# Trunk step: dispatch without the shift, shift added after the row turn, scatters issued back to back, and another layout for the last combination

## The reference

```python
mp = modulation(c_ctx[None, :], ada_w[l], ada_b[l])
ms = modulation(c, ada_w[l], ada_b[l])
...
hp = modulate(rms_norm(xp, norm_ffn[l]), mp[3], mp[4])
hs = modulate(rms_norm(xs, norm_ffn[l]), ms[3], ms[4])
xp = xp + mp[5] * hier_moe(hp, *moe)
xs = xs + ms[5] * hier_moe(hs, *moe)
```

## Time and profile before

| what | value |
|---|---|
| median of three runs | 1394.41 us |
| time of the profiled execution | 1396.16 us |
| its span | 1394.3 us |
| PE busy | 1235.7 us, 89% |
| DVE, ACT, POOL busy | 549.2, 380.5, 414.4 us |
| mean granted TensorE clock | 0.942 |
| DMA | 324.77 MB, mean 233 GB/s |

### The profile page before, as it was taken

One profiled execution on the slowest core, in us unless ns is written; L12 is line 12 of the kernel. 1 busy time (PEld: TensorE's weight loads), 2 busy tenths in 40 slices (PEclk: granted clock), 3 DMA queues, 4 the chain that ended last, 5 costly groups with the idle time before them and its releaser, 6 DMA issues.

```text
span 1394.3 us, 21214 instructions
## 1 busy us (share of the span) xinstructions
PE 1235.7 (89%) x7039; PEld 797.8 (57%) x7040; DVE 549.2 (39%) x1254; ACT 380.5 (27%) x779; POOL 414.4 (30%) x741
## 2 busy tenths in 40 slices
PE   6999998989989579998784899999999399999877
PEld 5666777655567345554443766665676255555437
DVE  3121424676622732222111449998213622222214
ACT  2210036556511311111110345664313011111110
POOL 0300100300000334453333159986001324445420
PEclk9999999989999779999997899999799599999998
DMA  9775653010036569999984911113552689999965
GB/s 379 269 255 210 260 216 134 3 61 1 1 39 233 228 261 411 423 424 423 423 356 173 273 58 38 57 61 102 116 205 112 261 334 408 369 421 423 423 247 227
DMA packets 104678, 324.77 MB, mean 233 GB/s; under 512 B 20405, under 2 KB 54171, under 8 KB 82083
## 3 DMA queue, kind: packets, MB, share of 16 engines
q1 hardware_dynamic: 84016, 290.36, 53.9%
q0 software_dynamic: 12464, 21.91, 4.4%
q10 hardware_dynamic: 8131, 11.59, 2.3%
HBM read 314.52 MB, written 27.10 MB: 245 GB/s over the span
## 4 chain that ended last, share of the span: by engine, by line
PE 65%; SPq 9%; DMA 9%; DVE 7%; issue 5%; ACT 2%; POOL 2%; ACTq 0%; POOLq 0%; DVEq 0%
PE PS L687 10%; PE PS L1043 10%; PE PS L1170 10%; PE PS L733 8%; PE PS L1065 5%; SPq L548 4%; DMA arena<-in_moe_w_up 4%; SPq L551 3%; PE PS L1111 3%; PE PS L640 3%; DVE scratch L1645 3%; PE PS L919 3%; DMA ring<-in_ada_w 2%; PE PS L1028 2%; DMA ring<-in_moe_w_up 2%
## 5 line engine op out<-in xcount | busy, mean ns | idle before, releaser
L1645 DVE TENSOR_TENSOR arena<-arena,PS 128x128 f32<-128x128 f32 (+3 forms) x109 | 40.3, 386 | 299.7 <-ACT arena L1540 288.8
L1043 PE MATMUL PS<-ring,arena 128*64 128x256 f32 x1088 | 132.3, 395 | 15.1 <-DMA ring<-in_moe_w_up 13.3
L733 PE MATMUL PS<-ring,arena 128*128 128x256 f32 (+1 forms) x640 | 143.3, 378 | 1.7 <-ACT arena L1352 1.7
L1170 PE MATMUL PS<-arena,ring 128*128 128x320 f32 x512 | 141.7, 438 | 3.5 <-issue 2.2
L1043 PE MATMUL PS<-arena 128*64 128x256 f32 x1120 | 130.6, 383 | 15.3 <-DMA arena<-in_moe_w_up 14.2
L2424 POOL TENSOR_TENSOR arena<-arena 128x655 f32<-128x655 f32 x91 | 129.7, 1425 | 45.2 <-ACT arena L1611 32.1
L687 PE MATMUL PS<-arena,ring 128*128 128x320 f32 x512 | 138.3, 433 | 4.8 <-DVE arena L1933 3.7
L733 PEld LDWEIGHTS PS<-ring,arena 128*128 128x128 f32 x640 | 116.3, 193 | 30.1 <-issue 15.3
L1170 PEld LDWEIGHTS PS<-arena,ring 128*128 128x128 f32 x512 | 97.7, 192 | 47.3 <-issue 8.6
L687 PEld LDWEIGHTS PS<-arena,ring 128*128 128x128 f32 x512 | 97.1, 190 | 45.6 <-issue 5.4
L2185 DVE SCALAR_TENSOR_TENSOR PS<-arena,vecT,PS 128x655 f32<-128x655 f32 x124 | 112.1, 904 | 4.2
(11 more groups left out here) (342 smaller groups left out, 1633.9 us busy)
## 6 DMA issues: line engine op xcount, KB each, us to landing
ring<-in_moe_w_up SPq DMA_DIRECT2D x64, 1024.0 KB, 15.1
arena<-in_moe_w_up SPq DMA_DIRECT2D x64, 1024.0 KB, 18.3
ring<-in_ada_w SPq DMA_DIRECT2D x48, 1024.0 KB, 9.0
ring<-in_moe_w_down SPq DMA_DIRECT2D x32, 1024.0 KB, 16.2
arena<-in_moe_w_down SPq DMA_DIRECT2D x32, 1024.0 KB, 18.5
arena<-y_rows ACTq DMA_DIRECT2D x10, 1024.0 KB, 8.0
ring<-in_od_w_in SPq DMA_DIRECT2D x16, 512.0 KB, 6.3
ring<-in_ev_w_in SPq DMA_DIRECT2D x7, 1024.0 KB, 15.6
```

The costliest lines, as they stand in the source:

```text
L733: last = pe.matmul(z_bank(i)[:, 0:n], hT[:, k, t * P:t * P + P], w[:, k, 0:n], start=(k == 0), stop=(k == KD - 1))
L1043: last = pe.matmul(PS[i * BLK:(i + 1) * BLK, 0, 0:2 * P].rearrange("p (a n) -> p a n", a=2), xblk[:, k, :], w[:, k % 4, :, i * P:(i + 1) * P],
L1170: last = pe.matmul(PS[:, 2 * a + n, 0:SEG], w[:, k, a, :], hT[:, k, n * SEG:(n + 1) * SEG], start=(k == 0), stop=(k == KD - 1))
L1645: return dve.tensor_tensor(out, a, b, op)
```

## The change

- *Dispatch.* Rows are sent without the latent shift, straight from ACT's `htok`. The latent shift, loaded as 128x8 values (`shift_x`), is added where DVE takes the turned rows (`take_rows`; one tensor_tensor for the copy). Context rows need the difference of the two shifts: DVE computes it (`shift_delta`), it goes to all partitions as one row (`delta_row`), and PE adds it to the context tile as a fifth product of its two halves, with a diagonal `cdiag` that ACT makes from the root. For these halves the turns become float32 products. POOL's five additions are gone.
- *Logits.* `router_bias` is gone. The two shift vectors stand as two more columns of `xA` (ACT copies them), pass with the raw logits, and two more selecting products give the biases; DVE forms `lbias` in the routing chain.
- *Scatters.* In POOL's loop the column copies come first, the gather no longer waits for the result block, and fewer small operations stand before a scatter. Before the last four scatters one copy takes all four columns, and the waits between them are gone.
- *First combination.* ACT squares by halves of a tile; POOL adds the eight chunks in three steps for four of the five tiles (the last is still summed by PE); sums, diagonals and spreads come one tile later in the order.
- *Last combination.* Tokens stay on partitions. PE turns `xT` while the results are awaited, and DVE copies it to `xout`, now in `ring`. Gate rows come through DRAM (`gate_rows`: two stores by element, two loads to all partitions). Per tile PE combines the lower 512 columns (two products of 512), ACT and DVE the upper ones, and DVE multiplies by the gate and adds.

The diff, cut to its core:

```diff
-            sp.wait_ge(ev("mod_c"), MODC + 5)
...
-                    .then_inc(ev("shift_dma"), 16)
+            sp.wait_ge(ev("coef"), DELTA[l])
+            for c, src in enumerate((modT[:, l, 24:24 + KD, 0], delta[:, l, :])):
+                sp.dma_start(shift_rows[2 * l + c].rearrange("(k p) -> p k", p=P), src,
+                             allow_slow_non_contiguous=True).then_inc(ev("shift_dma"), 16)
         if e == 2:
             sp.wait_ge(ev("shift_dma"), 64 * l + 32)
-            for c in range(2):
-                sp.dma_start(shift[c], shift_rows[2 * l + c].partition_broadcast(P)).then_inc(ev("shift_dma"), 16)
+            sp.dma_start(shift_x[:, :].rearrange("p (h m) -> p h m", h=2),
+                         shift_rows[2 * l].rearrange("(h p m) -> p h m", h=2, m=4)).then_inc(ev("shift_dma"), 16)
+            sp.dma_start(delta_row, shift_rows[2 * l + 1].partition_broadcast(P)).then_inc(ev("shift_dma"), 16)
         if e == NPLACE - 2:
             for t in range(NT):
-                sp.wait_ge(ev("h_tok"), NT * l + t + 1)
+                sp.wait_ge(ev("htok_a"), 2 * NT * l + 2 * (t + 1))
...
+for c in range(2):
+    sp.dma_start(gate_rows[c].rearrange("(k p) -> p k", p=P), modT[:, 1, 40:40 + KD, c],
+                 allow_slow_non_contiguous=True).then_inc(ev("shift_dma"), 16)
+sp.wait_ge(ev("down_mm1"), expert_done(EXPERTS - NPLACE))
+sp.wait_ge(ev("shift_dma"), 2 * 64 + 32)
+for c in range(2):
+    sp.dma_start(gate_row[:, c, :], gate_rows[c].partition_broadcast(P)).then_inc(ev("shift_dma"), 16)
 for s, t in enumerate(TILES):
-    sp.wait_ge(ev("xt_v"), 2 * NT + s + 1)
-    sp.wait_ge(ev("xt_a"), s + 1)
+    sp.wait_ge(ev("comb"), 2 * NT + s + 1)
...
-def router_bias(l, b):
...
-    last.then_inc(ev("shift_mm"), 1)
...
+            last = pe.matmul(PS[i:i + c, 2 * n, 0:SEG + 2 * n], wr_flat[:, ROUTE * k:ROUTE * k + c],
+                             xA[:, k, n * SEG:SEG + n * (SEG + 2)], start=(m == 0), stop=(m == KD // 2 - 1))
...
+        for c in range(2):
+            last = pe.matmul(PS[:, 6, (NT + c) * ROUTE:(NT + c + 1) * ROUTE], bc(rs[0:PAIR, T + c:T + c + 1], [PAIR, P]),
+                             cst[0:PAIR, C_SEL:C_SEL + ROUTE], start=True, stop=True)
...
+            rows = xA[:, 4 * half + j, cols(t)]
+            if t < ST:
+                last = pe.transpose(quad(b)[:, j, :], rows, ident)
+            else:
+                pe.matmul(quad(b)[:, j, :], rows, ident, start=(j == 0), stop=False)
+        if t == ST:
+            pe.wait_ge(ev("shift_dma"), 64 * (l + 1))
+            pe.wait_ge(ev("cdiag"), l + 1)
+            last = pe.matmul(PS[:, b, :], cdiag, delta_row[:, 512 * half:512 * half + 512], start=False, stop=True)
...
+        parts = KD if s == NT - 1 else 1
+        if parts == 1:
+            pe.wait_ge(ev("h_c"), SETUP + s + 1)
+        else:
+            pe.wait_ge(ev("squared"), KD + s + 1)
         if s >= 2:
             pe.wait_ge(ev("root"), ROOT[2] + s - 1)
-        for k in range(KD):
+        for k in range(parts):
             last = pe.matmul(PS[:, s % 2, 0:1], hT[:, k, cols(TILES[s])], ones[:, 0:1],
-                             start=(k == 0), stop=(k == KD - 1))
+                             start=(k == 0), stop=(k == parts - 1))
...
+    def turn_x():
+        for i in range(2 * NT):
+            t, half = i // 2, i % 2
             if i >= 4:
-                pe.wait_ge(ev(("xt_v", "xt_a")[i % 2]), (2 * NT if i % 2 == 0 else 0) + (i - 4) // 2 + 1)
+                pe.wait_ge(ev("xt_v"), 2 * NT + i - 3)
             for j in range(4):
-                last = pe.transpose(quad(i % 4)[:, j, :], xT[:, 4 * half + j, cols(TILES[s])], ident)
+                last = pe.transpose(quad(4 + i % 4)[:, j, :], xT[:, 4 * half + j, cols(t)], ident)
             last.then_inc(ev("x_t"), 1)
 
-    for s in range(NT + 2):
+    def combine_rows(s):
+        t = TILES[s]
+        pe.wait_ge(ring_full[SLOTS + t], back_full[l, t])
+        if s == 0:
+            pe.wait_ge(ev("wdiag"), 2 * NT * (l + 1))
+            pe.wait_ge(ev("xt_v"), 4 * NT)
+        if s == 4:
+            pe.wait_ge(ev("comb"), 2 * NT + 1)
+        for a in range(2):
+            last = pe.matmul(PS[:, 4 + s % 4, :], wdiag[:, a, t, :], ygat[:, t, a, 0:512],
+                             start=(a == 0), stop=(a == 1))
+        last.then_inc(ev("comb_mm"), 1)
+    if l == 1:
+        turn_x()
+        for s in range(NT):
+            combine_rows(s)
+        return
+    for s in range(NT + 3):
         if s < NT:
             combine(s)
-        if l == 0:
...
-            turn_out(s - 1)
+        if 2 <= s <= NT + 1:
+            tile_sum(s - 2)
+        if s >= 3:
+            spread(s - 3)
...
+        if k == 0:
+            act.activation(xA[:, :, T:TW], modT[:, l, 24:24 + KD, :], ACT.Copy)
...
+    act.wait_ge(ev("root"), ROOT[q])
+    act.activation(cdiag, ident, ACT.Copy, scale=ss[:, 1, ST:ST + 1]).then_inc(ev("cdiag"), 1)
...
+    for s in range(NT + 2):
         if s < NT:
-            act.wait_ge(ev("comb"), 2 * s + 2)
...
-            act.activation(ss[:, 1, s - 1:s], PS[:, (s - 1) % 2, 0:1], ACT.Sqrt, bias=eps, scale=1.0 / D) \
+            for half in range(2):
+                ks = slice(4 * half, 4 * half + 4)
+                act.wait_ge(ev("comb"), 2 * s + half + 1)
+                ins = act.activation(hT[:, ks, cols(TILES[s])], xT[:, ks, cols(TILES[s])], ACT.Square)
+            ins.then_inc(ev("squared"), 1)
+        if s >= 2:
+            act.wait_ge(ev("sumsq"), s)
...
+    act.wait_ge(ring_full[SLOTS + t], back_full[1, t])
+    act.activation(ygat[:, t, 0, 512:D], ygat[:, t, 0, 512:D], ACT.Copy, scale=wtok[:, 0, t:t + 1]) \
+        .then_inc(ev("xt_a"), 1)
...
+def shift_delta(l):
+    tt(delta[:, l, :], modT[:, l, 24:24 + KD, 1], modT[:, l, 24:24 + KD, 0], ALU.subtract).then_inc(ev("coef"), 1)
...
+    tt(lbias, PS[:, 6, NT * ROUTE:(NT + 2) * ROUTE].rearrange("p (c n) -> p c n", c=2),
+       bc(rb[:, l, :].unsqueeze(1), [P, 2, ROUTE]), ALU.add)
...
-        dve.tensor_copy(xblk.rearrange("p (c m) n -> p m c n", c=2),
-                        quad(3).rearrange("p m (c n) -> p m c n", c=2)).then_inc(ev(f"xblk_c{l}"), 1)
+        tt(xblk.rearrange("p (c m) n -> p m c n", c=2), quad(3).rearrange("p m (c n) -> p m c n", c=2),
+           bc(shift_x[:, :].rearrange("p (c m) -> p m c", c=2).unsqueeze(3), [P, 4, 2, BLK]), ALU.add) \
+            .then_inc(ev(f"xblk_c{l}"), 1)
...
+    def take_x():
+        for i in range(2 * NT):
+            dve.wait_ge(ev("x_t"), TURNED + i + 1)
+            dve.tensor_copy(xout[:, i // 2, 512 * (i % 2):512 * (i % 2) + 512], PS[:, 4 + i % 4, :]) \
+                .then_inc(ev("xt_v"), 1)
+        dve.wait_ge(ev("xt_v"), 4 * NT)
+        dve.wait_ge(ev("shift_dma"), 2 * 64 + 64)
+    def rows_out(s):
+        t = TILES[s]
+        c = 0 if t < ST else 1
+        lower, upper = ygat[:, t, 0, 0:512], ygat[:, t, 1, 512:D]
+        dve.wait_ge(ev("xt_a"), s + 1)
+        dve.scalar_tensor_tensor(out=upper, in0=upper, scalar=wtok[:, 1, t:t + 1], in1=ygat[:, t, 0, 512:D],
+                                 op0=ALU.mult, op1=ALU.add)
+        dve.wait_ge(ev("comb_mm"), 2 * NT + s + 1)
+        link(tt(lower, PS[:, 4 + s % 4, :], gate_row[:, c, 0:512], ALU.mult))
+        tt(upper, upper, gate_row[:, c, 512:D], ALU.mult)
+        link(tt(xout[:, t, 0:512], xout[:, t, 0:512], lower, ALU.add))
+        tt(xout[:, t, 512:D], xout[:, t, 512:D], upper, ALU.add).then_inc(ev("comb"), 1)
+    if l == 1:
+        take_x()
+        for s in range(NT):
+            rows_out(s)
+        return
+    for s in range(NT + 4):
         if s < NT:
             residual(s)
-        if l == 0:
...
-            turned_out(s - 2)
+        if 4 <= s:
+            normed_tile(s - 4)
+        if 3 <= s <= NT + 2:
+            tile_diag(s - 3)
...
-    pool.wait_ge(ev("shift_dma"), 64 * (l + 1))
...
-            .then_inc(ev("h_tok"), 1)
...
-    def columns(r, g, count, ahead):
...
-        settle(4 * r + 3)
     with pool.Fori(0, laps) as g:
         for r in range(LAND):
+            pool.tensor_copy(gather_col[:, r:r + 1], gather_at[:, bass.ds(4 * g + (2 * LAND + r + 2), 1)])
+            pool.tensor_copy(scatter_col[:, r:r + 1], scatter_at[:, bass.ds(4 * g + (LAND + r), 1)]) \
+                .then_inc(ev(f"column{l}"), 1)
             landed(r, g + 2)
             pool.wait_ge(ev(f"x_taken{l}"), 4 * g + (2 * LAND + r - 1))
+            pool.wait_ge(ev(f"column{l}"), 4 * g + (r + 1))
+            settle(4 * r + 2)
+            gather((r + 2) % LAND, gather_col[:, r:r + 1])
             pool.wait_ge(ev(f"yblk_c{l}"), 4 * g + (LAND + r + 2))
-            columns(r, g, 4 * g + (r + 1), True)
-            gather((r + 2) % LAND, gather_col[:, r:r + 1])
+            settle(4 * r + 3)
             scatter(r, scatter_col[:, r:r + 1])
             freed((r - 1) % LAND, g + (0 if r == 0 else 1))
+    for r in range(2):
+        landed(r, laps + 2)
```

(19 more changed lines are left out.)

102 lines of the change are left out of this document (31 added, 71 removed).

## The result

The changed kernel takes **1361.45 us** (median of 4 runs, 1360.37 to 1363.71), the kernel before, run beside it, 1394.74 (median of 4). The ratio is 0.9759, 95% interval 0.9738 to 0.9779: **33 us, 2.4%, faster**. The forecast was 1350.6 in a range of 1341 to 1363: faster, as forecast, but 10.8 us above the forecast time and near the slow end of the range, with a gain of 33 for 43.8. Most of the mechanisms hold; the price of item 1 doesn't, and two waits behind DMAs were left out.

A forecast was written before the change was run, and what follows sets the result against it. Weights were taken to bound the middle of the expert stages, compute their starts and the chain elsewhere. Savings of 43.8 us from 1396.16 left 1352.4, and 1.75 less for the median gave 1350.6, range 1341 to 1363.

The forecast's parts named there:

- item 1: Shift products, layer 0: taking them off PE saves 6.0 us, themselves and the queue behind them (ends 4.6 and 7.1).
- Item 2: Shift products, layer 1: removing them saves 7.0 us; lower end 5, as the output projection could start at the lower clock.
- Item 3: Routing: without POOL's additions DVE's operations run fast, 8.9 us saved per layer, 17.8 in all; dispatch not late next.
- Item 4: Expert blocks: DVE's take of turned rows, an add instead of a copy, costs zero; the gather's earlier start brings nothing.
- Item 5: Last scatters: fewer POOL operations and waits save 3.1 us in layer 0 (ends 1.5 and 4.5), 0.4 in layer 1.
- Item 6: First combination: fewer summing products on PE, most of it hiding a wait; 2.0 us saved (ends -1 and 4.5).
- Item 7: Last combination: turning done before the results land, shorter work per tile; 7.5 us saved (ends 3.5 and 9.2).
- A: First combination: DVE's diagonals wait for POOL's adds, so 2.0 saved becomes -2, total 1354.6 us; chance 0.12.
- B: Routing: something other than POOL slows DVE, so the 17.8 us stay, total 1368.4; chance 0.03.
- C: Expert stages: weights set their end, so the routing's 17.8 us and half the shift products' gain vanish, 1375; chance 0.04.
- D: Expert blocks: DVE's add runs far below the copy's rate in 69 blocks, slower, 1413 us at 2.8 beyond cover; chance 0.03.

## Why the prediction was right or wrong

**Item 1** (6.0; the stretch gained 6.4). Right only by the execution it was read from: "the difference, 5.9, is what L648 costs, itself and the queue behind it". The queue behind it was slow by the clock: 3.3 of the 5.5 us between the first latent and the first score product. The products cost 2.2, and 1.0 of the 6.4 comes later, between the first score product and the projection: 90.0 before, 89.0 after, and 88.8 to 89.6 in the other profiles without the products. That the stretch gained the forecast amount is luck.

**Item 2** (7.0). Right, 6.8, and 6.8 undone. The loss of 1.5 in the projection is the clock's chance, not, as its lower end feared, a consequence of the removed work.

**Item 3** (8.9 per layer; 8.3). The mechanism is right and shown by two runs; the term that was mis-sized is the lateness of ACT: its copies end 2.1 later for 1.4, and the wait for its exponential is 1.87 for 0.6. The step that failed is its last sentence, "the next late one is not the dispatch". It asked only whether SP's stores of rows end in time, and they do. Behind them stand 6 MB of weights of the last two places, issued by 473 and flowing until 486, and the gather shares the DMA engines with them. In the kernel before it came as they ran out, near 495.8. This took back 2.8 and 2.2, half of the shortfall of 10.8.

**Item 4** (0). Right: the take of the turned rows takes 0.69 (71 of them, 49.1 us in all). The sentence that the gather's earlier start is worth nothing was true for the loop only.

**Item 5** (3.1 and 0.4). Layer 0: 3.5 from the profiles, 3.6 undone. Layer 1: -0.8. The POOL operations taken out give the 0.4 (1.17 to 0.78 us from block to scatter), but it left out that the change's own gate rows go out then: from the last down product's end to the landing it is 12.5 us for 10.0. The stage ahead of it came out 1.8 shorter, within its spread.

**Item 6** (2.0). 0.9 in the profile, 3.7 when undone in the changed kernel; the last tile's sum at the lower clock took 3.2 for the 1.9 assumed.

**Item 7** (7.5). 7.6, and 7.7 undone. In part luck: from the landing to DVE's last operation it takes 19.8 us for the 19.1 laid out, a gain of 6.8, and the other 0.8 is the end behind that operation, 3.1 us for 3.8, which the sum left out. Its worry about the gate rows named the wrong victim: it had them land just before DVE asks for them, with 9 us for storing them (SP's issue alone takes 17.25), and didn't look at what travels beside them. 2.8 us of the last scatter's completion went.

**Rivals.** A (lock in the first combination): real, but not met in this change, where no diagonal starts within a POOL addition (the first, at 760.98, falls between one that ends at 760.43 and one that starts at 761.61); it appears as soon as all five tiles are added on POOL. The Trainium skill (SBUF — State Buffer, Who interferes with whom) named it, and its three kinds agree with the runs: tensor_tensor out of SBUF waits (1.96 for 0.32), tensor_scalar waits (0.85 for 0.29, one instance), tensor_reduce doesn't (0.17 to 0.20). That it made the sum smaller here by 4 is not borne out. B (routing stays slow): fell, and the returned additions show why. C (gains lost in the stream): fell in its form, the stages kept their length within their spread; but the weights did take 5 us, through the gather and not through the up products. D: fell.

The shortfall: gathers 5.0, clock in the two projections 3.2, routing 1.2, last scatter 1.2, first combination 1.1, item 2 0.2; against these 0.8 more than forecast in items 1 and 5 and 0.1 in item 7. That is 11.0 by the spans; the median lies 10.8 above the forecast. Of these, the gathers, the scatter and the routing are shown by runs that change them; the clock's part would come out otherwise with another pair of executions.

## What to carry to other kernels

When a step ahead of a transfer becomes faster, look at what is already in the DMA engines at the new time: a small gather amid prefetched weights took 6.5 us for 2.9, and holding back prefetches that PE needs some 30 us later was free here. Rows that are new must be stored and loaded in a stretch where the DMA engines idle, and never beside the transfer on the path. And a price for PE work that is read as a difference between two stretches of one execution should be compared by the granted clock of both before it is believed. In the same way a stage should be compared block by block before its length is put down to an edit: 29 of 36 blocks agreed to 0.1 us where two stages differed by 1.6.

## What the runs showed of the hardware that I had not expected

- The granted clock, with the same work on PE ahead, falls or stays from execution to execution: 1.5 to 1.7 us for a projection, 3.3 in and behind the shift products, 1.5 in the last weighted products. The profile of before was fast at both projections and in the weighted products, and slow behind the shift products.
- A DVE tensor_tensor of 0.20 us takes as long as the POOL instruction that it meets: up to 2 us beside pieces of 1.89, 0.3 to 0.8 beside pieces of 0.61. Cutting each of POOL's five instructions into four made the lists 2.5 us earlier, though POOL was busy for longer.
- A 256 KB scatter's completion doubles (2.6 to 5.5 us) beside 1 MB of broadcast rows that were issued 0.5 us before it; issued 1.7 us before, it takes 4.3.
